# Two-layer hybrid decoder step: norm roots of the first layer taken at once, tap matrices one per piece, last down groups of 7 and 4

## The reference, cut to what matters

```python
h = rmsnorm(x, norm1_g)
proj = einsum('btd,de->bte', h, w_in)               # 2048 -> 4352 columns
#   512 pooling, 3*768 short gated conv, 2*768 Conformer conv (GLU, depthwise conv of 31 taps)
mix = concatenate([y_pool, y_sconv, y_cconv])       # 2048
x = x + einsum('btd,de->bte', mix, w_out)
h2 = rmsnorm(x, norm2_g)
up = einsum('btd,df->btf', h2, w_up)                # 2048 -> 2*5632
up_c = causal_dwconv3(up)
act = silu(up_c[..., :D_FF]) * up_c[..., D_FF:]     # 5632
x = x + einsum('btf,fd->btd', act, w_down)          # 5632 -> 2048
```

## Time and profile before

| | us |
|---|---|
| time, median of 3 runs | 3146.94 (3145.32 to 3741.95) |
| the profiled execution's own time | 3147.87 |
| its span on the slowest core (core 3) | 3146.3 |
| spans of the eight cores | 3135.8 to 3146.3 |
| PE busy | 3066.6 (97%) |
| DVE / ACT / POOL busy | 1810.3 / 666.5 / 462.3 |

### The profile page before, as it was taken

One profiled execution on the slowest core, in us unless ns is written; L12 is line 12 of the kernel. 1 busy time (PEld: TensorE's weight loads), 2 busy tenths in 40 slices (PEclk: granted clock), 3 DMA queues, 4 the chain that ended last, 5 costly groups with the idle time before them and its releaser, 6 DMA issues.

```text
span 3146.3 us, 50359 instructions; the slowest of 8 cores (3135.8 to 3146.3 us)
## 1 busy us (share of the span) xinstructions
PE 3066.6 (97%) x19095; PEld 1638.2 (52%) x19095; DVE 1810.3 (58%) x2714; ACT 666.5 (21%) x830; POOL 462.3 (15%) x432
## 2 busy tenths in 40 slices
PE   5999999999999999999999999999999999999988
PEld 4455555555555555555555555555555555555545
DVE  4675633774475367357777663366537726744763
ACT  4111123220121022022241111232102202201213
POOL 0111111111111111111211111111111111111110
PEclk7999999999999999999999999999999999999999
DMA  8675677776876877786887668778687687768773
GB/s 173 93 112 60 69 68 66 70 69 63 73 69 63 74 71 64 70 77 63 87 103 107 76 64 69 67 66 72 61 76 69 61 74 70 69 62 76 72 102 124
DMA packets 820650, 243.44 MB, mean 77 GB/s; under 512 B 799140, under 2 KB 810780, under 8 KB 817820
## 3 DMA queue, kind: packets, MB, share of 16 engines
q0 software_dynamic: 741824, 191.13, 67.4%
q1 hardware_dynamic: 74304, 47.33, 6.1%
q10 hardware_dynamic: 4284, 1.77, 0.2%
HBM read 403.41 MB, written 17.15 MB: 134 GB/s over the span
## 4 chain that ended last, share of the span: by engine, by line
PE 89%; DMA 5%; DVE 3%; issue 2%; ACT 1%; SPq 0%; DVEq 0%; ACTq 0%; POOLq 0%
PE pB L397 43%; PE pA L397 41%; PE pB L693 2%; DMA sb_ar<-st_ffn 2%; DMA o_ffn_s<-sb_ar 2%; DVE sb_ar L413 1%; DMA sb_wr<-w_down 1%; PE pB L1011 1%; PE pA L1011 1%; DVE sb_mix L424 1%; DMA sb_mix<-xp 0%; PE pC L1011 0%; PE pC L514 0%; PE pA L574 0%; DVE sb_ar L424 0%
## 5 line engine op out<-in xcount | busy, mean ns | idle before, releaser
L397 PE MATMUL pA<-sb_hT,sb_wr 128*128 128x512 bf16 (+1 forms) x5856 | 1005.3, 331 | 2.9 <-DVE sb_ar L413 2.9
L397 PE MATMUL pB<-sb_hT,sb_wr 128*128 128x512 bf16 (+1 forms) x5856 | 999.6, 331 | 5.3 <-ACT sb_mix L433 4.0
L397 PEld LDWEIGHTS pB<-sb_hT,sb_wr 128*128 128x128 bf16 x5856 | 517.1, 98 | 465.6 <-issue 9.3
L397 PEld LDWEIGHTS pA<-sb_hT,sb_wr 128*128 128x128 bf16 x5856 | 517.4, 98 | 463.7 <-issue 7.5
L424 DVE SCALAR_TENSOR_TENSOR sb_ar<-sb_ar,sb_vecs 128x1056 f32<-128x1056 f32 x752 | 612.1, 833 | 163.0 <-ACT sb_ar L433 121.0
L433 ACT ACTIVATE sb_ar<-sb_ar,sb_vecs 128x1056 f32<-128x1056 f32 x352 | 258.8, 783 | 1159.3 <-DVE sb_ar L413 1156.6
L397 PE MATMUL pB<-sb_mix,sb_wr 128*128 128x512 bf16 (+1 forms) x2736 | 473.6, 331 | 8.0 <-DMA sb_wr<-w_down 8.0
L397 PE MATMUL pA<-sb_mix,sb_wr 128*128 128x512 bf16 (+1 forms) x2736 | 471.6, 330 | 0.0
L370 POOL DMA_DIRECT2D sb_wr<-w_up x176 | 200.9, 1141 | 1138.3 <-PE pA L397 570.8
L397 PEld LDWEIGHTS pB<-sb_mix,sb_wr 128*128 128x128 bf16 x2736 | 242.2, 98 | 225.0 <-issue 11.1
L397 PEld LDWEIGHTS pA<-sb_mix,sb_wr 128*128 128x128 bf16 x2736 | 241.7, 98 | 215.7 <-issue 1.1
(11 more groups left out here) (93 smaller groups left out, 996.7 us busy)
## 6 DMA issues: line engine op xcount, KB each, us to landing
sb_wr<-w_up POOLq DMA_DIRECT2D x176, 512.0 KB, 8.9
sb_wr<-w_in POOLq DMA_DIRECT2D x68, 512.0 KB, 7.9
sb_wr<-w_down POOLq DMA_DIRECT2D x96, 352.0 KB, 6.2
sb_wr<-w_out POOLq DMA_DIRECT2D x32, 512.0 KB, 8.6
sb_mix<-sb_ar SPq DMA_DIRECT2D x192, 67.8 KB, 4.8
sb_mix<-xp SPq DMA_DIRECT2D x8, 1024.0 KB, 14.2
yp<-sb_mix SPq DMA_DIRECT2D x8, 1024.0 KB, 3.9
sb_wr<-w_down POOLq DMA_DIRECT2D x32, 160.0 KB, 5.0
```

What stands on the lines that cost most here:

```text
L397: S.op("pe", lambda e, j=j, k=k, c0=c0, n=n: e.matmul(ps[:, c0:c0 + n], lhsT=wr[:, base + k, :], rhs=rhs_fn(k)[:, c0:c0 + n], start=(j == ...
```

## The change

It has four parts. (1) The x tiles' roots, reciprocals and diagonal matrices are done once for all ten tiles, by `x_rms(psn)`, which is put into the first chunk after its step 9: one root on ACT, one reciprocal on DVE, ten diagonal matrices on DVE (`dve_ts`) into tb[1], ten matmuls into the other PSUM tensor, one copy of 1184 columns on ACT to R0. The sums of squares stand side by side in ssq. (2) vecs is loaded in two: the 16 columns of n1g behind tile 0, the rest behind tile 3. (3) In layer 0 the tap matrices are built one in each piece. (4) In layer 1 the last two down groups are (33,7) and (40,4); layer 0 keeps (33,5) and (38,6).

```diff
-FG = [(0, 11), (11, 11), (22, 11), (33, 5), (38, 6)]
+FGS = [[(0, 11), (11, 11), (22, 11), (33, 5), (38, 6)], [(0, 11), (11, 11), (22, 11), (33, 7), (40, 4)]]
-    LASTF = FG[-1]
+    LASTF = FGS[-1][-1]
-    dgs = [Buf(OX + 896, 128), tailb[1]]
+    ssq = Buf(OX + 896, 16)
+    S.op("dve", lambda e: e.memset(ssq.ap, 1.0), writes=ssq.res)
     def x_turn(ti):
-        S.op("act", lambda e: e.activation(out=xjunk[0:n, :], in_=xi[0:n, :], func=AF.Square, accum_out=ss[0:n, :]),
-             reads=xr, writes=E[2].res + [("ss", ti)])
-        act(ss[0:n, :], ss[0:n, :], AF.Sqrt, [("ss", ti), "epsT"], [("ss", ti)], bias=epsT[0:n, :], scale=1.0 / D)
+        S.op("act", lambda e: e.activation(out=xjunk[0:n, :], in_=xi[0:n, :], func=AF.Square, accum_out=ssq.ap[0:n, ti:ti + 1]),
+             reads=xr, writes=E[2].res + ssq.res)
...
-            dve_tt(hT[:, half * 8:(half + 1) * 8, col0:col0 + n], xv, gv, ALU.mult, [("xt", ti, half), "vecs"],
+            dve_tt(hT[:, half * 8:(half + 1) * 8, col0:col0 + n], xv, gv, ALU.mult, [("xt", ti, half), "gain"],
-    def x_diag(ti):
-        S.op("dve", lambda e: e.reciprocal(out=ss[0:n, :], in_=ss[0:n, :]), reads=[("ss", ti)], writes=[("ss", ti)])
-        act(dg.ap[0:n, 0:n], identF[0:n, 0:n], AF.Copy, [("ss", ti), "identF"], dg.res, scale=ss[0:n, :])
-    def x_rms(ti):
-        ck = next_c()
-        S.op("pe", lambda e: e.matmul(pC[:, ck * 512:ck * 512 + n], lhsT=onesF.ap[0:n, :], rhs=dg.ap[0:n, 0:n], start=True, stop=True),
-             reads=dg.res + onesF.res, writes=[("pC", ck)])
-        act(R0[:, col0:col0 + n], pC[:, ck * 512:ck * 512 + n], AF.Copy, [("pC", ck)], ["R0"])
+    def x_rms(psn):
+        nt = len(tiles)
+        act(ssq.ap[:, 0:nt], ssq.ap[:, 0:nt], AF.Sqrt, ssq.res + ["epsT"], ssq.res, bias=epsT[:], scale=1.0 / D)
+        S.op("dve", lambda e: e.reciprocal(out=ssq.ap[:, 0:nt], in_=ssq.ap[:, 0:nt]), reads=ssq.res, writes=ssq.res)
+        ps = PS[psn]
+        for ti, (src, r0, n, col0) in enumerate(tiles):
+            dg = tb[1].ap[:, col0:col0 + n]
+            dve_ts(dg[0:n, :], identF[0:n, 0:n], ssq.ap[0:n, ti:ti + 1], ssq.res + ["identF"], [("dg", ti)] + (tb[1].res if ti == 0 else []))
+            S.op("pe", lambda e, dg=dg, n=n, col0=col0: e.matmul(
+                ps[:, col0:col0 + n], lhsT=onesF.ap[0:n, :], rhs=dg[0:n, :], start=True, stop=True),
+                reads=[("dg", ti)] + onesF.res, writes=[psn])
+        act(R0[:], ps[:, 0:T], AF.Copy, [psn] + tb[1].res, ["R0"])
     x_load(0)
-    S.op("sp", lambda e: e.dma_start(out=vecs[:], in_=vecs_d), writes=["vecs"], dma=True)
+    S.op("sp", lambda e: e.dma_start(out=vecs[:, 0:16], in_=vecs_d[:, 0:16]), writes=["gain"], dma=True)
     for ti in range(1, NXI):
         x_load(ti)
+    S.op("sp", lambda e: e.dma_start(out=vecs[:, 16:NV], in_=vecs_d[:, 16:NV]), writes=["vecs"], dma=True)
...
     for ti in range(len(tiles)):
-        if ti > 0:
-            x_diag(ti - 1)
         x_turn(ti)
         if ti + NXI < len(tiles):
             x_load(ti + NXI)
-        if ti > 0:
-            x_rms(ti - 1)
-    x_diag(len(tiles) - 1)
-    x_rms(len(tiles) - 1)
+    midq.append((9, x_rms))
...
-            if i == 0 and l == 0:
-                for k in range(6):
-                    taps_matrix(k)
+            if l == 0:
+                taps_matrix(i)
...
+        FG = FGS[l]
```

More of the change, by code:

```diff
@@ L564, in x_turn @@
         xi, xr = xin[ti % NXI], xin_res[ti % NXI]
-        ss = E[1].ap[:, 2 * ti:2 * ti + 1]
-        S.op("act", lambda e: e.activation(out=xjunk[0:n, :], in_=xi[0:n, :], func=AF.Square, accum_out=ss[0:n, :]),
-             reads=xr, writes=E[2].res + [("ss", ti)])
-        act(ss[0:n, :], ss[0:n, :], AF.Sqrt, [("ss", ti), "epsT"], [("ss", ti)], bias=epsT[0:n, :], scale=1.0 / D)
+        S.op("act", lambda e: e.activation(out=xjunk[0:n, :], in_=xi[0:n, :], func=AF.Square, accum_out=ssq.ap[0:n, ti:ti + 1]),
+             reads=xr, writes=E[2].res + ssq.res)
         for half in range(2):
@@ L585, in x_turn @@
             gv = V(("n1g", 0), half * 8, 8).unsqueeze(2).to_broadcast([128, 8, n])
-            dve_tt(hT[:, half * 8:(half + 1) * 8, col0:col0 + n], xv, gv, ALU.mult, [("xt", ti, half), "vecs"],
+            dve_tt(hT[:, half * 8:(half + 1) * 8, col0:col0 + n], xv, gv, ALU.mult, [("xt", ti, half), "gain"],
                    [("h", c) for c in range(half * 8, half * 8 + 8)])
-    def x_diag(ti):
-        src, r0, n, col0 = tiles[ti]
-        ss = E[1].ap[:, 2 * ti:2 * ti + 1]
-        dg = dgs[ti % 2]
-        S.op("dve", lambda e: e.reciprocal(out=ss[0:n, :], in_=ss[0:n, :]), reads=[("ss", ti)], writes=[("ss", ti)])
-        act(dg.ap[0:n, 0:n], identF[0:n, 0:n], AF.Copy, [("ss", ti), "identF"], dg.res, scale=ss[0:n, :])
```

## The result

The changed kernel takes 3119.8 and 3120.0 us, the kernel before 3145.3 and 3146.9 us on the same chip. The ratio is 0.9916 with a 95% interval of 0.9887 to 0.9945, so about 26 us less, between 17 and 36; the forecast of 3116.0 against 3146.9 was a ratio of 0.990. In the changed kernel L574 of before is L573, L693 is L685, and L1004, L1018 and L1011 are L996, L1010 and L1003.

A forecast was written before the change was run, and what follows sets the result against it. PE was taken as the bound, 89% of the chain, with gains only where it waits, runs slowly or does removable work: 13.1 + 7.6 + 11.1 = 31.8 us off 3147.87 gives 3116, range 3106 to 3129.

The forecast's parts named there:

- the last stage's: Last stage: two blocks fewer per tile save 17.3 us of work, less 0.8 us of new waits for DVE.
- the loads become the pace: First stage: without the diagonal matrix in the circle, x tile loads set the pace, 4.1 us a tile.
- ten pairs: First chunk: the norm's ten matmuls, each a pair of float32 passes, add 3.0 us.
- Rival (a): First stage: x loads don't come sooner, the last tile's takes 14.9 us; gain 5.2 us less, 3121; chance 0.15.
- tile 4 "at 28.1": First stage: tile 4 still lands at 28.1 us, because the moved vector load leaves the same bytes ahead.
- no wait above 1.5 us is left at piece 1: Layer 0's first Conformer pieces: a sign of being right, no wait for DVE at pieces 1 and 2 above 1.5 us.
- the cover in pieces 2 to 5: Layer 0: DVE's 2.65 us wait for ACT's sigmoid hides each piece's 1.15 us tap matrix; uncovered, four pieces lose 1.15 each.
- The 0.5 us that I put for the weight load: Last stages' group of 7 blocks: chunk 12's weights land just in time, 0.5 us allowed for waiting (ends 0 and 8).
- Rival (b): Group of 7 blocks: the weight wait stays, chunk 12 again 7.8 us short and slow for 2.6 after; 3126; chance 0.10.
- Rival (c): Group of 7 blocks: the weight queue becomes the bound, 15.4 us a load; slower than before, about 3189; chance 0.02.
- DVE still reads pA until 3093.74: Last stage: tiles shorten from 6.99 to some 5.2 us, so PE waits for DVE 0.2 us every second tile, 0.8 in all.
- Rival (d): First chunk: diagonal matrices late, piece 0's gate waits; a 5 us delay costs 3 us, 3119; chance 0.72 jointly with the forecast.

The follow-up runs named there:

- part 3 alone: The kernel before with only the tap matrices changed, one built in each piece of layer 0; ratio 0.9976 (0.9922 to 1.003).

## Where the prediction was right, and which of its steps failed

The forecast of 3116.0 us was 3.8 us low. Each part has the mechanism that was forecast; most of the miss is one term, the last stage's. The 3.8 us are also a net of errors both ways: +0.5 in the first stage, -0.7 in the pieces, -1.7 in the middle, +0.6 in the group and -2.4 in the last stage by the table, where plus is a larger gain than forecast. Part 4, forecast at 11.1 us, is 9.3 there and 7.1 in the means of the cores, where the group costs 7.0 us and not 4.8.

**Parts 1 and 2: right in the mechanism, with some luck in the number.** Forecast 53.5 us for the first chunk, measured 53.81; tile 9 forecast at 46.0 from the row of tile 6's load, measured 46.01. Two errors cancel in that 46.0. The load was to be issued at 36.2 and to take 9.7 us; SP issued it at 35.13 and it took 10.8. And PE was held by DVE until 45.69 anyway. The step "the loads become the pace" holds up to tile 4; behind it DVE is next, whose copy and products set 3.6 us a tile. The norm matmuls took 63.41 - 60.83 = 2.6 us where I put 3.0 for ten pairs, and the chunk is 2.3 longer than before. So 13.6 instead of 13.1.

Rival (a), which would have had the last tile 5.2 us later, is excluded by the start at 46.01. Its first half did come true: a load issued earlier waits longer. Tile 4's took 15.9 us after for 14.9 before, tile 6's 13.0 for 9.7. The Trainium skill's rule behind it (DMA: Bandwidth & Descriptors, Queues, rings and completion order) is not refuted by that. How much these loads lose to the weights' turns no run here shows, since the kernel that held weights back left their queue's traffic as it was. What the reasoning had not seen is the load of 700 KB that part 2 moved: I left tile 4 "at 28.1" as the same bytes stood ahead of it, and it is just these bytes that could be moved further, for 3 us of the stage.

**Part 3: right but for 0.7 us on this core, 1.5 in the mean.** Forecast 7.6, measured 6.9 (6.1 in the mean of the cores). Two steps are off. The first is that no wait above 1.5 us is left at piece 1: 1.96 us is, and the tap matmuls behind it are slow. The tap matrices are the cause of 1.3 to 2.8 us of it, by core: with all six built ahead the wait falls to 0.63 us and the stretch to 39.8 us. The 5.18 us of the tap matmuls don't come from the wait, since layer 1 takes 5.15 for them without a wait for DVE. The second is the cover in pieces 2 to 5. It holds, where four uncovered pieces would have added 4.6, but not to nothing: 0.3 to 0.5 us on every core, 0.7 with part 3 alone.

**Part 4: the group better than forecast on this core, the last stage worse.** The 0.5 us that I put for the weight load was nothing: it landed 2.4 us before PE asked for it, where 0.1 was forecast. The landing at 3051.55 that the sum was made from was one that the copies of SP had delayed; in the kernel before, moving them takes that load from 29.7 to 18.1 us. In the changed kernel the copies still run beside the twelfth chunk's load: SP issues them at 3011.43 and 3012.07 and its queue moves 2.4 MB from 3015 to 3033.6, and the load takes 28.5 us. So it isn't faster; it lands in time because PE, with chunks of 3.5 us, asks for it 11 us later after the group's start. Rival (b), whose case was the thin margin, didn't come. Rival (c) had priced the 11 us between two landings as the weight queue's own pace, where SP's queue was in the engines.

The step that failed is the last stage's: "DVE still reads pA until 3093.74 ... so PE waits about 0.2 us at every second tile, 0.8 in all". It gave 16.5 us and the stage gained 14.1. Over its pure work (69.35 - 17.3 us) the stage takes 3.2 us and not 0.8, and these 2.4 us are the whole of the term's miss. They come in two pieces:

- 1.66 us at the third tile, which starts 6.86 us after the second, where before it was 6.93 and two blocks less make 6.93 - 1.73 = 5.20 of that. The first root of the stage loads a table on ACT, 1.28 us, which tiles of 6.99 us had hidden and tiles of 5.2 don't; PE waits 1.50 us. The kernel that loads the table ahead shows it: there the distance is 5.59 us, and the stage is 1.5 us shorter. The prediction had no term for this load.
- 1.5 us in the seven distances behind it, of 5.23 to 5.58 us, where 0.8 was forecast for all. A tile that PE starts on DVE's release costs more than the wait shown: in the kernel with the table ahead, tiles with and without such a wait follow each other 5.59 and 5.23 us apart, 0.36 us and not 0.2, four times. Why it is more than the 0.23 us of the wait's row isn't shown.

The 1.7 us of the middle were forecast as 0. Some 0.8 of them are costs of the change (the pieces' cover and the wait near 266 us, each about 0.4); the rest differs by core.

Rival (d) is excluded by the row of the ten matrices: done at 56.23, asked for at 60.83.

## What to carry to other kernels

When an engine waits for a load, look at every queue that moves bytes in the ten microseconds before it lands, not only at the queue of the load: here copies that nobody waited for, on another queue, made a weight late, and moving two lines took away the wait that a new split of the work had taken away. When a stage gets shorter, list what its old length had covered, above all one-off work such as an ACT table load, and not only the steady pace. When an experiment holds traffic back, look at the queue's bytes in the stretch in question before reading its time: the traffic may not have changed there. And where a change moves a load "past" others with the same bytes in sum, ask which of these bytes the stage needs at all.
